# W_down product of a feed-forward layer: eight half-block products against seven, on one Trainium2 core

## The reference, cut to what matters

```
h2  = rmsnorm(x, norm2_gain) * (1 + scale2) + shift2          # 1024 x 1024
ffn = (silu(h2 @ w_gate) * (h2 @ w_up)) @ w_down              # hidden width 2816
x   = x + gate2 * ffn
```

## Time and profile before

| | |
|---|---|
| median of 3 runs | 991.25 us (990.68 to 992.0) |
| the profiled execution: its time | 991.97 us |
| its span in the profile | 990.2 us |
| granted TensorE clock | 0.998 |
| busy share | PE 98%, DVE 66%, ACT 38%, POOL 21% |

### The profile page before, as it was taken

One profiled execution on the slowest core, in us unless ns is written; L12 is line 12 of the kernel. 1 busy time (PEld: TensorE's weight loads), 2 busy tenths in 40 slices (PEclk: granted clock), 3 DMA queues, 4 the chain that ended last, 5 costly groups with the idle time before them and its releaser, 6 DMA issues.

```text
span 990.2 us, 13154 instructions
## 1 busy us (share of the span) xinstructions
PE 968.5 (98%) x4576; PEld 809.6 (82%) x4576; DVE 654.3 (66%) x1018; ACT 374.2 (38%) x715; POOL 206.7 (21%) x159
## 2 busy tenths in 40 slices
PE   7998999989999999999999999999999999999998
PEld 6887888878887778888888888888888888888886
DVE  3949999998689875646547456563556546655444
ACT  1335665576444743241423314233241422414220
POOL 0024555441100106120121212012120121202110
PEclk9999999999999999999999999999999999999999
DMA  9956644337244594334642445435334552345224
GB/s 358 378 185 239 221 150 149 107 145 274 93 128 149 175 330 167 137 128 170 212 170 85 170 153 185 169 132 189 141 131 169 192 189 85 136 163 210 85 85 170
DMA packets 84820, 170.88 MB, mean 173 GB/s; under 512 B 5440, under 2 KB 52272, under 8 KB 84784
## 3 DMA queue, kind: packets, MB, share of 16 engines
q1 hardware_dynamic: 79408, 158.95, 45.1%
q10 hardware_dynamic: 5376, 11.47, 3.3%
HBM read 155.32 MB, written 15.07 MB: 172 GB/s over the span
## 4 chain that ended last, share of the span: by engine, by line
PE 88%; DVE 5%; DMA 3%; ACT 2%; issue 1%; SPq 0%; POOL 0%; DVEq 0%; ACTq 0%
PE ps L1713 27%; PE ps L1715 27%; PE ps L1714 27%; DMA bs<-bs_scratch 1%; PE ps L1936 1%; DVE wi_lo L1312 1%; PE ps L1739 1%; DVE acc L1154 1%; PE ps L1819 1%; PE ps L1962 1%; PE ps L1746 1%; PE ps L1830 1%; DMA ada_in_raw<-in_w_ada 1%; DVE acc L1142 0%; DMA m_raw<-mixed_scratch 0%
## 5 line engine op out<-in xcount | busy, mean ns | idle before, releaser
L1552 DVE TENSOR_TENSOR x<-x,ps 128x512 f32<-128x512 f32 x176 | 120.7, 686 | 79.7 <-PE ps L1715 78.9
L1508 DVE TENSOR_TENSOR ring<-s,ring 128x512 fp32r<-128x512 f32 x88 | 73.9, 842 | 136.7 <-ACT ring L817 136.5
L1713 PE MATMUL ps<-h_hi,ring 128*128 128x512 f32 x352 | 137.2, 390 | 0.6 <-DVE h_lo L1501 0.6
L1715 PE MATMUL ps<-h_hi,ring 128*128 128x512 f32 x352 | 137.0, 389 | 0.0
L1714 PE MATMUL ps<-h_lo,ring 128*128 128x512 f32 x352 | 136.9, 389 | 0.0
L1713 PE MATMUL ps<-wd_hi,act_hi 128*128 128x512 f32 x352 | 136.9, 389 | 0.0
L1714 PE MATMUL ps<-wd_lo,act_hi 128*128 128x512 f32 x352 | 136.9, 389 | 0.0
L1715 PE MATMUL ps<-wd_hi,act_lo 128*128 128x512 f32 x352 | 136.9, 389 | 0.0
L1091 POOL TENSOR_TENSOR wd_lo<-raw_d,wd_hi 128x1024 fp32r<-128x1024 f32 x22 | 52.8, 2416 | 288.8 <-ACT wd_hi L863 288.8
L1086 POOL TENSOR_TENSOR raw_d<-raw_d,g2bc 128x1024 f32<-128x1024 f32 x22 | 59.1, 2710 | 225.3 <-DMA raw_d<-in_w_down 182.5
L1713 PE MATMUL ps<-bs,ring 128*128 128x512 f32 x264 | 103.0, 390 | 1.2 <-DVE h_lo L1501 0.7
(11 more groups left out here) (216 smaller groups left out, 1724.7 us busy)
## 6 DMA issues: line engine op xcount, KB each, us to landing
bs<-bs_scratch SPq DMA_DIRECT2D x126, 512.0 KB, 5.5
stage<-in_w_ada SPq DMA_DIRECT2D x24, 512.0 KB, 5.6
raw_g<-in_w_gate SPq DMA_DIRECT2D x11, 1024.0 KB, 5.2
raw_u<-in_w_up SPq DMA_DIRECT2D x11, 1024.0 KB, 7.3
raw_d<-in_w_down SPq DMA_DIRECT2D x11, 1024.0 KB, 8.7
ada_in_raw<-in_w_ada SPq DMA_DIRECT2D x16, 512.0 KB, 9.6
wi_raw<-in_w_in SPq DMA_DIRECT2D x8, 640.0 KB, 14.8
wo_raw<-in_w_out SPq DMA_DIRECT2D x8, 512.0 KB, 5.5
```

What stands on the lines that cost most here:

```text
L1508: dve.tensor_tensor(r[:, 1], a_source(m, o), r[:, 0].bitcast(F32), ALU.subtract).then_inc(a_lo, 1)
L1552: dve.tensor_tensor(xt, xt, bank(DB[j % 4]), ALU.add).then_inc(down_evac, 1)
L1713: pe.matmul(dst, s_hi, m_hi, start=start, stop=False, skip_group_check=onto)
L1715: return pe.matmul(dst, s_lo, m_hi, start=False, stop=stop, skip_group_check=onto)
```

## The change

The product with W_down is done by the same scheme, seven half-block products for eight. With the activation's blocks A11, A12, A21, A22 (128 hidden x 512 tokens; first index: token half) and W_down's B11, B12, B21, B22 (128 hidden x 512 columns), sums S1 = A21+A22, S3 = A11-A21, S2 = S1-A11, S4 = A12-S2 and T1 = B12-B11, T3 = B22-B12, T2 = B22-T1, T4 = B21-T2 are built, and split into two parts each. The 512 tokens of a half are done in 4 rows of 128, two rows in each of two groups g; each (row, product) is one `mm3` of three matmuls with its own semaphore count: 28 parts a pair.

- DVE builds the activation's four sums (`act_sum`) and seven low parts (`act_low`, before: four) at the start of the next pair's front products; ACT makes seven high parts.
- POOL scales `raw_d` as before, but later: `load_down(p)` now waits until down(p-1) is over, and is two DMAs of 512 KB. Then POOL makes three low parts, four sums (`sums_down`), four more low parts, all 128x512, and adds P5 to x1 (8 operations a pair, `add_p5`) from ACT's copies.
- ACT copies partial sums from bank to bank and to SBUF (12 copies a pair: `copy_x`, `copy_y`, `copy_v`).
- DVE adds the rest to x1 straight from PSUM (16 a pair); the sum U3 stays in its bank, DVE adds it to C22 and PE then accumulates P4 on it for C21.
- The front order is A11, S2, A12, S3; S2 multiplies with a fourth streamed block T2 (`bs_dram` has 4 blocks), which frees a part of h_hi/h_lo for the activation's sums. SP waits for `bs` chunk by chunk.
- In the last pair W_down is prepared by DVE (`prepare_last`, `sums_last`), ACT and POOL in buffers of its own, and group 0 has another order.

```diff
@@ SP
             def load_stream(p, n, first=False):
+                src = bs_dram[(STREAMED.index(T2), STREAMED.index(T3), STREAMED.index(T4), STREAMED.index(B22))[n]]
...
+            def load_down_half(p, q, dst=None):
+                sp.dma_start((raw_d if dst is None else dst)[:, q, :], wd_d[bass.ds(p * 2 * P + q * P, P), :]).then_inc(rd_in, 16)
             def load_down(p, first=False):
                 if not first:
-                    sp.wait_ge(wd_lo_done, 2 * p)
...
+                    sp.wait_ge(down_chain, 2 * NSTEP * p)
+                load_down_half(p, 0)
+                load_down_half(p, 1)
...
             def pair_loads(p, last=False):
                 load_stream(p, 0)
-                load_down(p)
...
+                load_stream(p, 1)
...
                     load_raw(p + 1, 0)
                     load_raw(p + 1, 1)
...
+                load_stream(p, 2)
...
+                    load_down(p)
+                    load_stream(p, 3)
@@ ACT
+            def copy_x(p, g, j):
+
+                act.wait_ge(down_chain, step(p, g, ("P1a", "P1b")[j]))
...
+                    act.wait_ge(down_evac, 16 * p + 5 + j)
+                act.activation(bank(YB[j]), bank(XB[j]), ACT.Copy).then_inc(copied, 1)
...
             def second_half(p, par, last=False, first=False):
...
+                act_high(D_A22, p)
+                if not first and not last:
+                    down_high(W_B11, p)
+                    down_high(W_B21, p)
+                    down_high(W_B22, p)
                 silu_in_place(u2s, p, 3)
                 if not last:
...
+                    a_high(p + 1, S2, 0, 1 - par)
             def first_half(p, par, second=False):
 
+                a_high(p, S2, 1, par)
                 copy_p1(p, 0)
...
+                sum_high(D_S1, p - 1)
+                sum_high(D_S3, p - 1)
                 copy_p1(p, 1)
...
+                sum_high(D_S2, p - 1)
+                a_high(p, A12, 0, par)
+                sum_high(D_S4, p - 1)
+                a_high(p, A12, 1, par)
+                copy_u(p, S2, 0)
+                down_high(W_T1, p - 1)
+                down_high(W_T3, p - 1)
                 a_high(p, S3, 0, par)
@@ POOL
+            def sums_down(p):
+
+                pool.wait_ge(wd_lo_done, 7 * p + 3)
+                pool.tensor_tensor(raw_b(0, 0), raw_b(0, 1), raw_b(0, 0), ALU.subtract).then_inc(w_sum, 1)
+                pool.wait_ge(w_sum, 4 * p + 1)
+                pool.tensor_tensor(raw_b(0, 1), raw_b(1, 1), raw_b(0, 1), ALU.subtract).then_inc(w_sum, 1)
...
+            def prepare_down(p, first=False):
+
+                scale_down(p)
...
+                for b in (W_B11, W_B21, W_B22):
+                    low_down(b, p)
+                sums_down(p)
+                for b in (W_T1, W_T3, W_T2, W_T4):
+                    low_down(b, p)
+
+            def add_p5(p, g, j):
+
+                pool.wait_ge(v_copied, 4 * p + 2 * g + j + 1)
+                for t in (HALF1[2 * g + j], HALF0[2 * g + j]):
+                    pool.tensor_tensor(x1_half(t, 1), x1_half(t, 1), p1s[j][:, :], ALU.add).then_inc(pool_evac, 1)
...
+            with pool.Fori(1, NPAIR - 1) as p:
+                adds_down(p - 1)
+                prepare_down(p)
@@ DVE
             def second_half(p, par, last=False):
...
                 gate(p1s[1][:, :], p1s[0][:, :], bank(GB[1]), p, 2)
                 a_low(p, S4, 1, par)
-                act_low(p1s[1][:, :], 1, 0, p, 2)
+                act_low(D_A12, p)
                 if not last:
                     a_sum2(p + 1, 0)
...
             def first_half(p, par, last=False):
 
-                a_low(p, S2, 0, par)
+                act_sum(D_S1, p - 1)
                 a_low(p, S2, 1, par)
+                act_sum(D_S3, p - 1)
+                act_sum(D_S2, p - 1)
+                act_low(D_S1, p - 1)
+                act_low(D_S3, p - 1)
+                act_sum(D_S4, p - 1)
+                act_low(D_S2, p - 1)
+                a_low(p, A12, 0, par)
+                act_low(D_S4, p - 1)
+                a_low(p, A12, 1, par)
...
+                add_c11(p - 1, 0, 0)
+                add_c11(p - 1, 0, 1)
                 a_low(p, S1, 0, par)
                 a_low(p, S1, 1, par)
...
+                adds_back(p - 1, 0)
+                if not last:
+                    a_sum13(p + 1, 0)
+                add_c11(p - 1, 1, 0)
+                add_c11(p - 1, 1, 1)
@@ PE
+            def products_front(p, par):
+
+                for m in range(2):
+                    pe.wait_ge((silu_done, gated_done)[m], 4 * p - 3)
                     product(p, A11, m, par, GA, True, FIRST, 0)
...
                 for m in range(2):
                     pe.wait_ge(p1_copied, 2 * p + m + 1)
+                    stream_product(p, S2, m, par, GB, 0)
+                for m in range(2):
                     product(p, A12, m, par, GA, False, FIRST, KT // 2)
...
+            def down(p, last=False):
+
+                def part(name, dst, d, b, i, start):
+                    u = slice(i * P, (i + 1) * P)
+                    mm3(dst, D_HI[d][:, u], D_LO[d][:, u], W_HI[b], W_LO[b], start, True, not start).then_inc(down_chain, 1)
...
+                        if g == 1:
+                            pe.wait_ge(down_evac, 16 * p + 7)
...
+                        part("P5a", bank(ZB[0]), D_S1, W_T1, a, True)
...
+                    pe.wait_ge(copied, 8 * p + 4 * g + 1)
+                    part("P2a", bank(XB[0]), D_A12, W_B21, a, False)
...
             def pair_step(p, par):
...
+                products_front(p, par)
                 down(p - 1)
...
+                streamed_products(p, A22, par, GB, 2)
+                pe.wait_ge(down_evac, 16 * p)
+                products_back(p, par)
```

More of the change, by code:

```diff
@@ L851, in silu_in_place, with act_high @@
                 act.activation(buf[0][:, :], buf[0][:, :], ACT.Silu).then_inc(silu_done, 1)
[L853 to L863, removed]
+            def act_high(d, p):
+                act.wait_ge(gated_done, 4 * p + d + 1)
+                act.activation(D_HI[d], D_RAW[d], ACT.Copy).then_inc(acthi_done, 1)
@@ new lines, in copy_v, with copies_front @@
+            def copy_v(p, g, j):
+                act.wait_ge(down_chain, step(p, g, ("P5a", "P5b")[j]))
+                if g == 0:
+                    act.wait_ge(actlo_done, 7 * p + 7)
+                else:
+                    act.wait_ge(pool_evac, 8 * p + 2 + 2 * j)
+                act.activation(p1s[j][:, :], bank((ZB, XB)[j][0]), ACT.Copy).then_inc(v_copied, 1)
+            def copies_front(p, g):
+                copy_x(p, g, 0)
+                copy_x(p, g, 1)
+                copy_v(p, g, 0)
@@ L964, in second_half @@
                 a_high(p, S4, 1, par)
-                act_high(p1s[1][:, :], 1, 0, p, 2)
-                if not last:
+                act_high(D_A12, p)
+                if last:
+                    for b in range(7):
+                        down_high(b, p, True)
+                else:
                     a_high(p + 1, A11, 0, 1 - par)
@@ L1082, in scale_down, with low_down @@
             def scale_down(p):
-                pool.wait_ge(rd_in, 16 * p + 16)
                 for q in range(2):
+                    pool.wait_ge(rd_in, 32 * p + 32)
                     pool.tensor_tensor(raw_d[:, q, :], raw_d[:, q, :], g2bc[:, :], ALU.mult).then_inc(wd_scaled, 1)
[L1088 to L1092, removed]
+            def low_down(b, p, last=False):
+                pool.wait_ge(wd_hi_done, 7 * p + b + 1)
+                if b == W_B11 and not last:
+                    pool.wait_ge(wd_scaled, 2 * p + 2)
+                if b in (W_T1, W_T3, W_T2) and not last:
+                    pool.wait_ge(w_sum, 4 * p + 4)
+                pool.tensor_tensor(W_LO[b], (W_RAW_LAST if last else W_RAW)[b], W_HI[b].bitcast(F32), ALU.subtract).then_inc(wd_lo_done, 1)
@@ L1094, in _, with adds_down @@
+            def adds_down(p):
+                for g in range(2):
+                    add_p5(p, g, 0)
+                    add_p5(p, g, 1)
             pool.wait_ge(g2_done, 1)
             pool.wait_ge(a_sum, summed(1, S2, 1))
[L1096 to L1102, removed]
+            prepare_down(0, first=True)
@@ L1614, in _ @@
             gate(silu_sb, silu_sb, bank(GA[1]), 0, 1)
[L1615 removed]
+            act_low(D_A11, 0)
             take_gate2()
@@ L1685, in first_half @@
                 a_sum4(p, 1)
+                add_c11(p - 1, 0, 0)
+                add_c11(p - 1, 0, 1)
                 a_low(p, S1, 0, par)
                 a_low(p, S1, 1, par)
-                for j in range(NT * NH):
-                    add_down(p - 1, j)
-                    if j == 10:
-                        act_low(silu_sb, 0, 0, p, 1)
-                    if j in (8, 12) and not last:
-                        a_sum13(p + 1, j // 4 - 2)
+                adds_back(p - 1, 0)
[3 more added lines that the diff above has]
+                add_c11(p - 1, 1, 1)
+                if last:
```

(7 more changed lines are left out.)

434 lines of the change are left out of this document (304 added, 130 removed).

## The result

The changed kernel takes 1019.33 us (median of 4, 1016.56 to 1021.48); beside it the kernel before took 991.62. The ratio is 1.028, 95% interval 1.025 to 1.031: slower by 27.7 us, where I had forecast 11 to 12 and a range up to 1016. Direction and places were right, the size was too small by 16 us. First the page of the profile after: busy time by engine, then the shares of the last chain, to be read beside the earlier trace rows.

The account below looks back on a forecast made before the run. PE was taken to bound the kernel, busy 98% of the span. -29.9 + 19 + 16 + 3 + 3.5 + 0.5 = +12.1 us on 991.97 gave 1004.1 us (1003 on the median); 8-in-10 range 965 to 1016.

Parts of the forecast that it names:

- The gain: In down, 84 matmuls a pair instead of 96, at pitch 0.2267 us over 11 pairs: 29.9 us less.
- Stall 1: Before S4, POOL's later scaling holds up DVE's operations: 2.1 us a pair in pairs 1 to 9, 19 us (11 to 25).
- E: Time mark in a pair: the end of A22 on PE; PE wants S4 at E+5.44.
- Stall 2: In the front, POOL's low parts and sums alternate with DVE: S2 m=1 1.8 us late, nine times, 16 us (5 to 23).
- Q: Time mark: the start of the next pair; PE wants S2 m=1 at Q+8.16.
- the upper price: In the front, POOL's 128x512 operations taken at 1.2 us instead of 1.04: A12 late too, 2.55 us.
- The last pair and the end: Down(10) has no products to hide behind; late operands, C21 adds and final stores together cost 3.5 us (2 to 6).
- Pair 1: W_down prepared later, between pairs 0 and 1, so copy_p1 and later operands come late: 3 us (1 to 5).
- Costed at nothing: Copies inside down, DVE's 16 adds, POOL's 8 adds, fourth stream, later loads and ACT's load, all expected to add no time.
- the three signs that I would be wrong: Scaling starting 2 us or more before E, DVE's two-input operations keeping 0.69 us beside POOL, PE waiting inside down for ACT.
- all hidden: Rival: alternation finds room or raw_d lands early enough, so the loop's stalls vanish; -26, 965 us; chance 0.20.
- The stalls feed on each other: Rival: a late C12 add also holds P5a of group 1, both long stalls at upper ends; 1025 us; chance 0.10.

Follow-up runs that it names:

- run 9: Kernel of run 8 with S3's operand made earlier on ACT and DVE, and C21's two additions moved ahead in the last pair: 977.12 us, ratio 0.985.
- Run 3: Kernel before the change, with only raw_d of pairs 1 to 9 loaded and scaled at the new, later time: 1016.47 us, ratio 1.025.
- run 7: Changed kernel with POOL's four sums of a pair cut to 128x1, so T1 to T4 are not formed: 1008.16 us, ratio 1.017.
- run 2: Changed kernel with ACT's copy_p1 of m=1 put ahead of the high parts of S1 and S3: 1024.12 us, ratio 1.033.
- run 8: Changed kernel with scaling split, take_sum, copy_p1 and both A12 operands earlier, last pair's scaling behind adds_back: 992.95 us, ratio 1.001.
- run 5: Changed kernel with only DVE's order altered, take_sum of u3s ahead of a_sum2 and the A11 low part: 1020.38 us, ratio 1.029.
- run 1: Changed kernel with POOL's two scaling operations of a pair cut from 128x1024 to 128x1: 987.99 us, ratio 0.996.
- run 6: Changed kernel with only POOL's scaling split, four operations of 128x512 for two of 128x1024: 1019.75 us, ratio 1.028.

## Why the prediction was right in sign and short in size

- **The gain** held: 132 matmuls fewer, pitch 0.2267 where nothing waits, and 57.24 us a pair once the waits are gone (run 9).
- **Stall 1** held in mechanism and nearly in size: 21.5 us for 19. POOL was forecast to start at E-0.1; by the starts of the nine scalings it was from E-0.5 to E+1.4. Where it began at E-0.5 (the pair shown) PE lost 1.9 us, where it began at E+0.9 2.6, and 3.1 at E+1.4. Run 3 shows this term alone, 18.7 us. Also, `take_sum` ended at E+7.1 in the pair shown, for E+7.5.
- **Stall 2** held in mechanism, and its sum came out right, 14.3 us, by errors of both signs. Forecast 16; measured in pairs 2 to 10: 10.0 before S2 m=1 and 4.3 before A12. The 128x512 operation of POOL, for which the shortest of the earlier trace rows gave me 1.04 us, takes 1.27 where nothing holds it (two in 2.54) and 1.62 in the alternation; half of the 128x1024 one, 1.2, was the nearer guess. The alternation's pitch was 1.70 against my 1.64, and gate 4 got through at Q+3.0 instead of 3.7. So `copy_p1` ended at Q+9.2 for Q+9.95, and A12's operand, which I had late only at the upper price, was late in fact. Runs 7 (cause) and 2 (same cause, next operand) show it.
- **The step that failed**, and with it the size: the sum priced each stall at PE's idle time, and PE's work behind it at the full speed ("pitch still 0.2267"); for what a wait does to the matmuls behind it there was no term, and no reason was given for leaving it out. The runs show two surcharges. Late second matmuls and small restarts took 5.6 us (0.5 before), and half-speed stretches 3.8 us in this execution and 4.5 to 14.4 in runs 2, 3 and 7. Together 8.9 of the 15 us by which the profiled execution missed the sum; stall 1 gives 2.5 and the last pair with the end 3.7. With the surcharges alone put in, the sum would have been 1013 us for 1019.
- **The last pair and the end** were mis-sized: 3.5 forecast, 4.9 of waits and 2.3 of tail measured. C21's second addition made P5a of group 1 wait 2.3 us, for 1.0: DVE's C22 addition in group 0 was held for POOL's `add_p5` (1.5 us idle before 999.07), a queue that I hadn't followed. One more wait, 1.3 us at 969.29, is for C22's addition of down(9), which stood on DVE behind the scaling of `prepare_last` (4.57 us from 964.07); run 8, with that scaling behind `adds_back`, doesn't have it. At the end two stores of 512 KB start at 1010.20 and the next two at 1011.46; DVE's last addition ends at 1012.03, and the kernel 4.9 us later.
- **Pair 1**: 3 forecast, 2.9 before S2 m=1 and about 0.9 at A12, 3.8.
- **Costed at nothing** and at nothing: the copies inside down and the fourth stream, which none of PE's waits behind 340 us names. ACT is named, but only at `copy_p1`, where it had itself waited for DVE. None of the three signs that I would be wrong occurred: scaling didn't start 2 us before E, DVE's two-input operations didn't keep 0.69 us, and PE didn't wait inside down for ACT's copies.
- **The rivals**: "all hidden", 965 us, is what the kernel becomes with other orders: 977 in run 9. What lies between is mostly what PE still loses in pair 1 (5.2 us) and around the last pair (4.3), and 7.4 us behind the last matmul. "The stalls feed on each other" was the nearest in number (1025), but not by its mechanism: no P5a of a pair in the loop waited, and what came on top of the stalls was the late restarts and the clock. Runs 5 and 2 do show a coupling of another kind: work put off at one group is missing at the next.

What stays open: how the saving of 31 us in run 1 divides into the shorter front and the clock, since both go with the scaling; and the 5.6 us of late second matmuls are counted, not explained.

## What to carry to other kernels

An engine busy for 54% of a pair can still stop the bound engine, if its instructions hold up another that is making something on the path: look at which two engines work in the last microseconds before each operand is due, and put the operand first in *both* queues, ahead of all that is wanted later. Mending one such place alone moved the wait (1020 and 1024 us for 1019); four places together gave the whole gain in the loop of pairs. And price a stall of 2 us of TensorE above its idle time, since what follows it can run at half speed.

## What the hardware showed that I had not expected

- **The clock behind waits.** Half-speed matmuls came in stretches of 5 to 13, at a pitch of 0.43 us. Behind 340 us in the eleven traces each such stretch begins within 1.7 us of the end of a wait of 1.9 to 4.6 us, and the kernel before, with no wait of over 0.9 us in this part, has none. Not every long wait brings one: of the nine waits before S4 two did in the changed kernel, three in run 3 and eight in run 7. That the waits are the cause is argued from this, not tested by itself.
- **Alternation has a pitch of its own.** A 128x512 operation of POOL (1.27 us alone) and one of DVE (0.60) alternate every 1.70 us, less than the sum of 1.87. Halving POOL's instructions (run 6) gave 1.9 us a wait instead of 2.4 and no time.
